# Four RMS norms in front of projections: the root applied after the matmuls instead of before the transposes

## The reference, cut to what matters

```python
def rms_norm(x, g):
    xf = x.astype(jnp.float32)
    y = xf * lax.rsqrt(jnp.mean(xf * xf, axis=-1, keepdims=True) + EPS)
    return (y * g.astype(jnp.float32)).astype(x.dtype)
...
x = _parallel_mixer_layer(x, ...)   # norm 0, attention + state-space mixer, added to x
x = _swiglu_ffn(x, ...)             # norm 1; silu(h @ w_gate) * (h @ w_up) @ w_down, added to x
x = _short_conv_layer(x, ...)       # norm 2; three projections b, c, v; conv(c * v) * b @ w_out
x = _swiglu_ffn(x, ...)             # norm 3, as norm 1
x = _rmsnorm(x, final_norm)         # norm "first"
h = rms_norm(x, attn_norm)          # norm 4, then the projections of fox and sliding attention
x = x + hybrid_mixer(h, ...)
h = rms_norm(x, ffn_norm)           # norm 5, then 64 experts
```

## Time and profile before

| what | value |
|---|---|
| median of 3 runs | 1940.18 us (1938.21 to 1940.57) |
| the profiled execution's own time | 1940.26 us |
| its span, first to last instruction | 1938.5 us |
| PE busy | 1772.5 us (91%) |
| DVE, ACT, POOL busy | 1478.4 us (76%), 1215.2 us (63%), 122.8 us (6%) |
| mean granted TensorE clock | 0.973 of full speed |

### The profile page before, as it was taken

The page is one execution under the profiler, slowest core; times in us unless marked ns, Lnnn a source line. Parts: engine busy times, 40 slices in busy tenths (PEclk is TensorE's granted clock), DMA queues, the critical chain, the costliest instruction groups (busy, mean ns, idle before and its releaser), DMA issues.

```text
span 1938.5 us, 26082 instructions
## 1 busy us (share of the span) xinstructions
PE 1772.5 (91%) x10364; PEld 1540.1 (79%) x10364; DVE 1478.4 (76%) x1181; ACT 1215.2 (63%) x954; POOL 122.8 (6%) x134
## 2 busy tenths in 40 slices
PE   6996899989899998989899899999999989999896
PEld 6975799989799987977777777777777777777775
DVE  4767545567555455446689999999999999999997
ACT  4454434443333334535388888888888888888885
POOL 1245000000000000332000000000000000000000
PEclk9998999999999998998799999999999999999999
DMA  6420345464334454431589999999999999999993
GB/s 260 189 87 1 131 163 195 174 248 164 131 131 178 179 192 150 170 141 75 197 367 428 423 417 418 413 429 412 419 423 411 429 412 419 420 409 429 412 421 162
DMA packets 40644, 544.12 MB, mean 281 GB/s; under 512 B 4624, under 2 KB 4752, under 8 KB 5904
## 3 DMA queue, kind: packets, MB, share of 16 engines
q1 hardware_dynamic: 40592, 543.39, 69.1%
HBM read 542.32 MB, written 1.05 MB: 280 GB/s over the span
## 4 chain that ended last, share of the span: by engine, by line
PE 54%; DVE 19%; issue 14%; ACT 9%; POOL 2%; DMA 0%; DVEq 0%; POOLq 0%; ACTq 0%; SPq 0%
PE psum L893 13%; DVE ring_r L2001 12%; PE psum L767 9%; ACT arena_r L1555 7%; PE psum L903 6%; PE psum L1210 5%; PE psum L1181 5%; PE psum L802 4%; PE psum L1195 4%; PE psum L785 2%; PE psum L1220 2%; PE psum L1145 1%; POOL arena L2171 1%; DVE x L2098 1%; PE psum L838 1%
## 5 line engine op out<-in xcount | busy, mean ns | idle before, releaser
L2001 DVE TENSOR_TENSOR ring_r<-ring,arena_r 128x4096 fp32r<-128x4096 f32 x192 | 846.0, 4421 | 39.2 <-ACT arena_r L1555 34.9
L1555 ACT ACTIVATE arena_r<-ring 128x4096 fp32r<-128x4096 f32 x182 | 660.8, 3631 | 0.0
L1181 PE MATMUL psum<-arena_r,stream_r 128*128 128x512 f32 x1024 | 412.4, 403 | 34.9 <-DVE ring_r L2001 26.0
L1181 PE MATMUL psum<-ring_r,stream_r 128*128 128x512 f32 x1024 | 401.8, 392 | 0.0
L1181 PEld LDWEIGHTS psum<-arena_r,stream_r 128*128 128x128 f32 x1024 | 193.5, 189 | 92.4 <-DVE ring_r L2001 26.4
L1770 DVE TENSOR_TENSOR ring_r<-ring,arena_r 128x3072 fp32r<-128x3072 f32 x40 | 134.3, 3359 | 161.5 <-ACT arena_r L1374 161.5
L1374 ACT ACTIVATE arena_r<-ring 128x3072 fp32r<-128x3072 f32 x40 | 111.0, 2774 | 193.8 <-DMA ring<-in_ffn 193.8
L1181 PEld LDWEIGHTS psum<-ring_r,stream_r 128*128 128x128 f32 x1024 | 193.5, 189 | 38.1
L893 PE MATMUL psum<-stream_r,arena_r 128*128 128x256 f32 x704 | 200.7, 285 | 6.2 <-DVE arena_r L1643 6.2
L893 PE MATMUL psum<-stream_r,ring_r 128*128 128x256 f32 x704 | 200.4, 285 | 0.0
L893 PE MATMUL psum<-arena_r 128*128 128x256 f32 x704 | 200.4, 285 | 0.0
(11 more groups left out here) (298 smaller groups left out, 2535.9 us busy)
## 6 DMA issues: line engine op xcount, KB each, us to landing
ring<-in_w SPq DMA_DIRECT2D x192, 2048.0 KB, 10.4
ring<-in_ffn SPq DMA_DIRECT2D x44, 1536.0 KB, 6.4
ring<-in_w_in SPq DMA_DIRECT2D x8, 2048.0 KB, 8.3
ring<-in_in_w SPq DMA_DIRECT2D x7, 2048.0 KB, 13.0
ring<-in_out_w SPq DMA_DIRECT2D x7, 2048.0 KB, 8.1
ring<-in_l_in SPq DMA_DIRECT2D x8, 1536.0 KB, 8.6
ring<-in_proj SPq DMA_DIRECT2D x2, 2048.0 KB, 7.7
ring<-in_misc SPq DMA_DIRECT2D x1, 1632.0 KB, 8.5
```

The costliest lines, as they stand in the source:

```text
L1181: last = mm(dst, xg[:, k, :], b[:, k * D_EXPERT:(k + 1) * D_EXPERT], start=(k == 0 and b is u_hi), stop=(k == KD - 1 and b is u_lo))
L1555: A(w_hi[u % HI_SLOTS], ring[:, MOE_SLOT[at], :], ACT.Copy).then_inc(m_hi, 1)
L2001: V.tensor_tensor(ring_r[MOE_SLOT[u % NM]][:, :], raw, w_hi[u % HI_SLOTS].bitcast(F32), ALU.subtract).then_inc(m_lo, 1)
```

## The change

For norms 1 to 4 PE transposes `x` itself, half a chunk at a time, as soon as that half is added (`residual_T`); the gain goes into the copies as before (for norm 4 the product of the two gains, `gain4`). The root is computed meanwhile, spread by two small matmuls over all partitions (`spread_root`), and multiplied into what the projection gives. The first weight tile is taken feature block by feature block (`project_pair`), each block waiting only for its own low half (`f_low`).

```diff
+            def residual_T(n, name):
+                for j in range(4):
+                    begin(f"norm{n}_{j}")
+                for tc, h in RES:
+                    pe.wait_ge(*O.drained(f"{name}_{tc}{h}"))
+                    for k in range(4 * h, 4 * h + 4):
+                        at = k % 2 * T + tc * P
+                        last = nc.tensor.transpose(bank(f"norm{n}_{k // 2}")[:, at:at + P], x[:, tc, k * P:(k + 1) * P], ident)
...
+            def project_pair(dst, n_norm, u, columns_of):
+                for k in range(KD):
+                    pe.wait_ge(f_low, n_norm * KD + k + 1)
+                    for m in range(2):
+                        for i, (a, w) in enumerate(hi_lo_passes(xnT_r, XN_LO[n_norm], *u)):
...
+            def spread_root(n):
+                begin(f"root{n}")
+                if n == 4:
+                    pe.wait_ge(root12_ready, 1)
+                else:
+                    pe.wait_ge(rstd_ready, NT * (NORMS[n] + 1))
...
+                for tc in range(NT):
+                    last = mm(bank(f"root{n}")[:, tc * P:(tc + 1) * P], root[:, tc:tc + 1].to_broadcast([P, P]), ident,
...
+                pe.wait_ge(*S.low(f"ffn{n}_0"))
+                project_pair(gu[0], 2 * n + 1, unit(0, s[0]), lambda k, m: (m * KD + k) * P).then_inc(ffn_in, 1)
+                pe.wait_ge(*S.low(f"ffn{n}_1"))
+                spread_root(2 * n + 1)
```

In the short convolution the order on PE is `cv0` as a pair, `spread_root(2)`, `b0`; behind norm 4 it is `fq0` as a pair, `fq1`, `fk0`, `spread_root(4)`, `fk1`. On ACT:

```diff
-            square(1, added("out0"))
-            ffn(0, "l1_0")
-            square(2, added("ffn0"))
-            split("l1_1")
-            norm_T_hi(2)
+            ffn(0, "out0", "l1_0")
+            norm_T_hi(2)
+            split("l1_1")
+            square(2, added("ffn0"))
```

On DVE, in `norm_lo` and in `hidden`:

```diff
-                    last.then_inc(dve_drained, 1)
+                                               xnT_r[:, k, :].bitcast(F32), ALU.mult, ALU.subtract).then_inc(f_low, 1)
+                    dve.wait_ge(f_low, n * KD + 2 * j + 2)
+                    V.engine_nop().then_inc(dve_drained, 1)
...
+                    dve.wait_ge(ffn_in, j)
+                    V.tensor_tensor(gate_n[:, b, :], gu[b][:, 0, :], ffn_root, ALU.mult).then_inc(ffn_scaled, 1)
                     dve.wait_ge(ffn_silu, j)
-                    V.tensor_tensor(h_f[:, b, :], sg_f[:, b, :], psum[:, (base + b) % 8, T:2 * T],
-                                    ALU.mult).then_inc(h_made, 1)
+                    V.tensor_tensor(h_f[:, b, :], sg_f[:, b, :], gu[b][:, 1, :], ALU.mult).then_inc(h_gated, 1)
+                    dve.wait_ge(h_gated, j)
+                    V.tensor_tensor(h_f[:, b, :], h_f[:, b, :], ffn_root, ALU.mult).then_inc(h_made, 1)
```

In the loop `hidden(i, b)` now stands ahead of the low half of unit b + 2. In the short convolution the copy of `c` is now a multiplication by the root squared, and `sc_conv` gets one more multiplication, by the root. On DVE at norm 4:

```diff
+            norm_lo(4)
             scaled_norm("first", x_final, 16)
-            norm_lo(4)
             split("fk")
+            dve.wait_ge(rstd_ready, NT * (NORMS[4] + 1))
+            V.tensor_tensor(root12, rstd[:, NORMS["first"], :], rstd[:, NORMS[4], :], ALU.mult).then_inc(root12_ready, 1)
             split("fv")
```

More of the change, by code:

```diff
@@ L111, in add, with emptied_as, hold @@
         self.info.append((name, drainer, self.n, self.count[drainer]))
-    def skip(self):
+    def emptied_as(self, *names):
+        counts = sorted(self.info[self.at[name]][3] for name in names)
+        for name, k in zip(names, counts):
+            tile = self.info[self.at[name]]
+            self.info[self.at[name]] = (tile[0], tile[1], tile[2], k)
+    def hold(self, name):
+        self.at[name] = len(self.info)
         self.info.append(None)
@@ L427, in plan_attention @@
                 if t < len(others):
-                    O.add(others[t], "act")
+                    O.add(others[t], drainer)
                 if 2 <= t < len(items) + 2:
@@ L444, in plan_ffn @@
             plan_norm(2 * n + 1)
+            for b in range(2):
+                O.hold(f"gu{n}_{b}")
+            O.add(f"root{2 * n + 1}", "dve")
             plan_out(f"ffn{n}")
-            O.skip()
-            O.skip()
         plan_norm(0)
@@ L483, in program @@
             O.add(f"cv{j}", "dve")
+            if j == 0:
+                O.add("root2", "dve")
             O.add(f"b{j}", "dve")
+        O.emptied_as("root2", "cv0")
         plan_out("out1")
@@ L487, in program @@
         plan_norm(4)
-        for n in ("fq", "fk"):
-            for j in range(2):
-                O.add(f"{n}{j}", "act" if j == 0 else "dve")
+        for name in ("fq0", "fq1", "fk0", "root4", "fk1"):
+            O.add(name, "dve")
+        O.emptied_as("root4", "fq0", "fq1", "fk0")
         for tc in range(NT):
@@ L749, in norm_T @@
                 for tc in range(NT):
-                    pe.wait_ge(xn_ready, NT * n + tc + 1)
+                    pe.wait_ge(xn_ready, tc + 1)
                     turn_rows(n, xn, tc)
+            def residual_T(n, name):
[6 more added lines that the diff above has]
+                        last = nc.tensor.transpose(bank(f"norm{n}_{k // 2}")[:, at:at + P], x[:, tc, k * P:(k + 1) * P], ident)
+                        if tc == NT - 1 and k % 2 == 1:
+                            end(f"norm{n}_{k // 2}", last)
             def normed(n):
-                for j in ((3,) if n in SPLIT_NORMS else (2, 3)):
+                for j in (2, 3):
                     pe.wait_ge(*O.drained(f"norm{n}_{j}"))
@@ L930, in _ @@
             norm_T(0)
-            normed(0)
+            pe.wait_ge(f_low, KD)
             for tc in range(NT):
@@ L1089, in _ @@
                      [(sc_split, kc + 1) for kc in range(KD)])
-            ffn(1)
-            norm_T(4)
-            normed(4)
-            for n in ("fq", "fk"):
-                for j in range(2):
-                    channels(f"{n}{j}", n, 2 * j, 4)
+            ffn(1, "out1")
+            residual_T(4, "ffn1")
+            u = halves("fq")
+            begin("fq0")
+            end("fq0", project_pair(bank("fq0"), 4, u, lambda k, m: k * 512 + m * P))
+            channels("fq1", "fq", 2, 4)
+            channels("fk0", "fk", 0, 4)
+            spread_root(4)
+            channels("fk1", "fk", 2, 4)
             for tc in range(NT):
@@ L1308, in norm_T_hi @@
                         k = 2 * j + kk
-                        last = A(xnT_r[:, k, :], bank(f"norm{n}_{j}")[:, kk * T:(kk + 1) * T], ACT.Copy, scale=c(GAIN[n], k))
+                        last = A(xnT_r[:, k, :], bank(f"norm{n}_{j}")[:, kk * T:(kk + 1) * T], ACT.Copy, scale=gain(n, k))
                     last.then_inc(x_high, 1)
@@ L1325, in copy, with nothing @@
                 A(dst, src, func).then_inc(act_drained, 1)
+            def nothing():
+                pass
             def attention(kinds, others):
@@ L1508, in _ @@
             for tc in range(NT):
-                copy(f"sq{tc}", rope_x[:, tc, 0:512])
+                act.wait_ge(*O.ready(f"sq{tc}"))
+                scaled(f"sq{tc}", tc, rope_x[:, tc, 0:512], 0, 512).then_inc(act_drained, 1)
             split("gs0")
@@ L1524, in _ @@
             copy("skT", skT[:, :, :])
-            attention(["fox", "swa"], [lambda j=j: copy(f"gs{j}", gates[:, 1, 2 * j:2 * j + 2, :]) for j in range(4)]
-                      + [lambda: split("pf")])
+            attention(["fox", "swa"], [nothing] * 4 + [lambda: split("pf")])
             split("ps")
@@ L1685, in nothing, with attention @@
                 pass
-            def attention(kinds, mask_of, dst_of, others=()):
+            def attention(kinds, mask_of, dst_of, others=(), tiles=()):
                 def masked(kind, u):
@@ L1779, in _ @@
             dve.wait_ge(x_in, 16)
+            norm_rows(0)
+            split("misc")
             norm_lo(0)
```

189 lines of the change are left out of this document (114 added, 75 removed).

## The result

The changed kernel takes 1918.86 us (median of 4 runs, 1915.12 to 1921.21), the kernel before 1940.38 in its four; the ratio is 0.9887, 95% interval 0.9874 to 0.9899. It is faster by some 21.5 us where 31.9 were forecast, and 0.9 us outside the range. The profiled execution took 1919.65 us, its span is 1917.9.

What follows compares the result with a forecast made beforehand. PE bounds the kernel, busy 1772.5 of 1938.5 us, with waits at the norms. Gains 7.3 + 7.4 + 6.3 + 12.1, less 1.4, 0.1 and 0.3, plus 0.6, make 31.9: 1940.2 to 1908.3 us, range 1902 to 1918.

Steps and rivals of the forecast that it cites:

- the loops run in steps of exactly 8.5: Feed-forward loops: added VectorE work fits the slack, steps of 8.5 us, 0.6 us gained over both layers, bounds 0 and 1.5.
- the wait at the end of ffn1: Last unit of feed-forward 1: three more instructions in the chain, PE waits 2.3 instead of 0.88 us, loss 1.4.
- the self-waits: VectorE's waits for its own low-half blocks: 0.1 us each, bounds 0 and 0.2; four at norm 0 lose 0.3.
- Norm 4: Tiles fq0 to fk1 end at A + 28.3 against A + 40.38, with a 0.8 wait for `fk`'s low half; gain 12.1 us.
- A: Start of the first of a norm's four additions on VectorE; the forecast's times at that norm count from it.
- what the forecast put at nothing there: Attention: first mask about 0.9 us late, inverted sums waiting for `gs{j}`; uncovered, 0.9 and about 0.7 a unit for four units.
- the first rival: Slow clock stays, now in each norm's first tile, costing 1.7 us per norm partly covered by waits; total 1911, chance 18%.
- squares at A + 8.3, POOL a microsecond later: Norms 1 and 3: ScalarE's squares end at A + 8.3, GpSimd's root a microsecond later, early enough for unit 1.
- root A + 12.3: Norm 2: root matmuls end at A + 12.3 after PE waits 2.0 us; the stage's gain was put at 6.3.
- take the clock to stay at 1.00: Norm 1: with PE's longest pause about 1 us, the granted clock stays full; the sum is then 1908.
- a pause of 3 brings the fall: Norm 1 before the change: PE's two 3 us pauses bring half clock, and transposes help against it.
- that of the late queues: Queues behind the copies later than forecast, or attention gives back part: 2 to 3 us at three places, 1916, chance 11%.

Runs made afterwards that it cites:

- experiment 2: Changed kernel with ScalarE's two squares at norm 2 put ahead of the second projection tile's rounding; 1914.26 us, ratio 0.9838.
- Experiments 1, 2 and 7: The last of the three numbers: the changed kernel measured again, 1917.93 us, and on the same chip with all mends in one, 1903.88 us.
- experiment 1: Changed kernel with VectorE's subtraction for the second weight tile's low half issued in four pieces at norms 1, 2 and 3; 1912.26 us, ratio 0.9839.
- experiment 4: Changed kernel with 24 unused matmuls of 256 columns on TensorE in front of norm 2's root; 1912.82 us, one run.
- `b1_norm0`: Changed kernel with norm 0's roundings put back as before, without waits for each pair; 1910.71 us, one run.
- `b2_before_again`: The kernel before, unchanged, profiled a second time; first addition of norm 1 at 223.76 us, chip's median for the kernel before 1942.19 us.
- `c1_all`: Changed kernel with norm 0 as before, norm 2's squares first, `fq`'s subtraction in four pieces, ffn0/ffn1 second-tile subtractions in six, root ahead of the low-half wait; 1903.88 us.
- `d1_all_again`: The same kernel as `c1_all`, the changed kernel with all mends, a second time; 1904.62 us, ratio 0.981.
- experiment 3: Changed kernel with `fq`'s low-half subtraction at the end of ffn1 in four pieces, two before the last hidden tile and two behind; 1912.45 us, ratio 0.9843.
- `d2_all_but_norm0`: Changed kernel with all mends of `c1_all` except that of norm 0, whose waits for each pair stay in; 1904.49 us, ratio 0.9815.

## Why the prediction was right and where it was wrong

Right, by its own steps: PE starts after the low part of the first block (4.25 for 4.1); the loops run in steps of exactly 8.5 and gain 0.44 (ffn0; units 0 and 1 to norm 2's additions take 174.13 instead of 174.57); the hidden values of unit 0 cost nothing; the wait at the end of ffn1 is 2.25 for 2.3; the self-waits, put at 0.1 each with no row for them, took that (eight low blocks 3.62 us, where 3.23 stood). Norm 4 is right to 0.2 where the clock stays (fv starts 28.1 after the first addition in experiment 2, 28.3 forecast; 29.5 in the changed kernel, whose first addition lies inside the slow product), but partly by luck: PE starts at A + 4.4 for 4.1 and the pair takes 5.99 for 5.75, while the wait of 0.8 for the low half of `fk` did not come (it is ready at A + 15.9, and fq1 ends at A + 16.2). From fv to norm 5 the two profiles take 179.3 before and 179.5 after, so what the forecast put at nothing there shows no loss. But in other profiles with the change this stretch takes 177.5 to 182.2, so a loss under some 2 us could hide in it. The clock in the first tile of each norm stayed at 1.00, so the first rival, a slow stretch there, did not come.

**The step that failed** is "squares at A + 8.3, POOL a microsecond later", and with it "root A + 12.3" at norm 2. POOL's second multiply-add starts at A + 7.9, and DVE's subtraction, which the change puts right beside it, holds it until A + 10.7. Experiments 1, 2 and 7 show this: the hold shrinks with the size of DVE's instruction (2.82, 0.41 and 0.75) and goes when no subtraction runs. At norms 1 and 3 the root takes the place of the low half as the last to come, and PE starts unit 1 at A + 12.15 and A + 12.25 instead of A + 11. About 0.8 of that is the hold: the low half is there at A + 10.6, as forecast, and PE starts on the root at A + 11.5. The rest is mainly the root's matmuls, 0.68 where 0.3 to 0.4 was put for them. At norm 2 they end at 431.10, A + 14.2 instead of A + 12.3, 1.9 us: the hold costs 2.0 (POOL is done at 430.26, and would be at about 428.25 with 0.19 and 0.55 behind the squares), the matmuls and the hand-over 0.4, and the squares end 0.5 earlier than forecast.

This could have been read from the kernel before. Timelines of DVE and POOL at its norm 4:

```profile
726.31 1.29 DVE L1653 SCALAR_TENSOR_TENSOR x<-x,stat,norm_row 128x1024 f32<-128x1024 f32 x1 [0.79 <-POOL stat L2156]
...
726.79 0.86 POOL L2155 TENSOR_SCALAR stat<-stat 128x1 f32<-128x1 f32 x1 [0.61 <-ACT xn L1290]
```

L2155 is the same multiply-add, 0.19 us when alone. It starts inside DVE's instruction and ends at 727.65, when that one does (727.60). The forecast took POOL's time as fixed, wherever it lands.

The Trainium skill, "SBUF — State Buffer", section "SBUF: two separate sides", says that VectorE and GpSimd share one pair of ports, that a VectorE instruction with two SBUF inputs and a GpSimd instruction that reads SBUF exclude each other there, and that whoever starts first keeps the pair for the whole instruction. The instructions here are of those kinds, and the trace agrees: 2.83 us for 0.19. The runs show the exclusion; that it is the ports, no run here shows. In experiment 1 the holds are 0.2 to 0.6 us, under a piece's 0.9, as when a POOL instruction comes in the middle of a piece.

**The second step that failed** is "take the clock to stay at 1.00". It was said of norm 1 and is right there, but it was carried to norm 2, where the forecast itself had a pause of 2.0, and to the end of ffn1 with 2.3. Behind norm 2's 3.25 us the clock fell each time, at 1.5 us (experiment 4, which changes nothing but that pause). Behind the 2.25 of ffn1 it fell in five profiles of seven, at about 1.4 (200.34 against 198.88). The step "a pause of 3 brings the fall" drew a line between 3 and 2.3 from the two pauses of one profile. The runs show no such line: the clock fell behind 2.25 us and stayed behind 2.57 (experiment 1). The Trainium skill, "TensorE: Matmul & The Clock Gate", Part 1, says that the chip judges activity by a measurement that runs on by itself, so that the moment of a change differs between runs of one kernel. The seven profiles fit that: one program, one pause, two outcomes.

Norm 2 lost by both, 1.9 + 1.5: 6.3 became 2.8. With the squares first the stage gains 7.25 over before (102.68 to 95.43), one more than forecast.

**The rest** is where the clock falls in the first and the last stage, which the change touches only at norm 0 and in norm 5's transposes. The first addition of norm 1 stood at 221.23, 223.76 and 222.86 in three profiles of before, at 221.12 to 226.02 in four with norm 0 as before, and at 223.54 to 226.19 in seven with its waits. The forecast took one profile of before as the kernel; its first stage was the fastest of the three by 1.6 us. How much of the 3.6 us in the first stage is such luck is not settled: the means are 222.6, 223.7 and 224.7, the spreads 2.5 to 4.9, and 0.4 is norm 0's. What speaks for luck is that profiles of like clock agree with and without the change, once norm 0 is as before: 221.23 (before) and 221.12 (`b1_norm0`) with a mean granted clock of 0.95 over the stage, 223.76 (`b2_before_again`), 223.89 (`c1_all`) and 223.72 (`d1_all_again`) with 0.93. But 226.19 (experiment 3) has 0.93 too, so the mean clock alone does not give the time.

The last stage was 994.3 to 996.1 before and 991.8 to 997.7 in eleven others, and there the clock settles it. Windows of PE alone over its first 50 us, before, changed, and `d2_all_but_norm0`:

```profile
942.38:992.38 50.00, 44.08 (x212) 0.76 0.49 193
...
920.41:970.41 50.00, 43.92 (x198) 0.73 0.46 178
...
910.05:960.05 50.00, 43.88 (x230) 0.86 0.56 225
```

The stages behind these clocks take 996.1, 997.5 and 991.9. All fourteen profiles keep this order: 0.86 goes with 991.8 to 992.2, 0.83 with 993.7, 0.80 with 994.3, 0.76 with 995.8 to 996.2 (two of before and four of changed ones), 0.73 with 997.5 to 997.7. So the 1.4 us lost here are the clock's, and norm 5's transposes cost nothing that shows.

The range failed because the cases were taken one by one. The result, 1918.9, lies beyond both the clock's rival (1911) and that of the late queues (1916), because a piece of each came true at once: from 1908.3, the 6.6 us missing in the touched stages alone make 1914.9. And the spread of the first and the last stage, 2 us and more to either side, was not in the range at all.

## What to carry to other kernels

When a change moves a small GpSimd instruction beside a large VectorE one with two inputs, cost it at the end of the large one, or cut that one into pieces; here such pieces and the order of two instructions on ScalarE were worth 7 of the 14 us between the changed kernel and the mended one (1.45 at norm 1, about as much at norm 3, 4.4 at norm 2). Of the rest some 3 are the pause at the end of ffn1 and its clock, and most of what is left is where the clock fell elsewhere. When a wait takes the place of another, ask for each how long TensorE stands still, and add the slow clock behind it as likely, not as excluded. Here it came behind ten of twelve pauses of 2.25 or 3.25 us. And profile the kernel before twice: what differs between two profiles of one kernel is no ground for a forecast.

## What the runs showed of the hardware that was not expected

- A 128x1 multiply-add on GpSimd took 0.19 us alone and 2.82 inside a VectorE subtraction of 3.35; VectorE showed no delay (3.35 before the change and after it). Cutting the subtraction into four or six pieces made it 3.56 and 3.69.
- 24 matmuls of 256 columns with no use, in a pause of 3.25 us, kept the granted clock at 1.00 and gained 1.5 us.
- A pause of TensorE of 2.25 us at the same place was followed by half clock in five profiles and by full clock in two.
